# A ring of expert weights cut into 22 half-matrix tensors instead of 11 whole ones

## What is computed

```python
def routed_experts(xf, expert_idx, gates, w1, w3, w2):
    ...                      # sort the 1024 (token, expert) pairs by expert
    def expert_block(args):
        xb, e = args
        return (jax.nn.silu(xb @ w1[e]) * (xb @ w3[e])) @ w2[e]
    ...                      # gate, and add each token's two results
def hierarchical_moe(h, router_group, router_expert, w1, w3, w2):
    ...                      # top 1 of 4 groups, then top 2 of its 8 experts
    return routed_experts(xf, expert_idx, gates, w1, w3, w2).reshape(b, t, d)
```

## Time and profile before

| | |
|---|---|
| median of 3 runs | 2085.11 us (2085.02 to 2099.13) |
| the profiled execution | 2079.74 us, of which the span from first to last instruction is 2078.0 us |
| granted TensorE clock, mean | 0.905 of full speed |
| PE / PEld busy | 1707.9 us (82%) / 945.1 us (45%) |
| DVE / ACT / POOL busy | 678.9 us (33%) / 421.1 us (20%) / 173.4 us (8%) |
| HBM read / written | 461.24 MB / 23.46 MB |
| SP's queue (q1) | 86688 packets, 454.97 MB |

### The profile page before, as it was taken

One profiled execution on the slowest core, in us unless ns is written; L12 is line 12 of the kernel. 1 busy time (PEld: TensorE's weight loads), 2 busy tenths in 40 slices (PEclk: granted clock), 3 DMA queues, 4 the chain that ended last, 5 costly groups with the idle time before them and its releaser, 6 DMA issues. The chain is left out here.

```text
span 2078.0 us, 22342 instructions
## 1 busy us (share of the span) xinstructions
PE 1707.9 (82%) x8688; PEld 945.1 (45%) x8817; DVE 678.9 (33%) x1098; ACT 421.1 (20%) x725; POOL 173.4 (8%) x205
## 2 busy tenths in 40 slices
PE   7999679998794998888888499988949888888883
PEld 5775268886442333333333267854423333333331
DVE  5432966666613111111111353296221111111113
ACT  5224322222511110000000232274101100000001
POOL 0001611221101000000000100054010000000001
PEclk9999789998797999999999799999979999999996
DMA  5301000002085999999999632012759999999994
GB/s 163 102 21 21 1 1 1 1 1 82 6 325 203 360 408 405 406 407 401 405 398 399 227 106 81 15 68 60 317 216 377 399 405 403 410 403 405 396 386 167
DMA packets 99722, 486.18 MB, mean 234 GB/s; under 512 B 30912, under 2 KB 55488, under 8 KB 74528
## 3 DMA queue, kind: packets, MB, share of 16 engines
q1 hardware_dynamic: 86688, 454.97, 56.0%
q0 software_dynamic: 4736, 17.17, 2.2%
q10 hardware_dynamic: 8192, 12.59, 1.9%
HBM read 461.24 MB, written 23.46 MB: 233 GB/s over the span
## 5 line engine op out<-in xcount | busy, mean ns | idle before, releaser
L617 PE MATMUL ps<-w_unit,xT 128*48 128x512 f32 x1024 | 513.1, 660 | 132.5 <-DMA w_unit<-in_moe_w 129.9
L618 PE MATMUL ps<-w_unit,xT 128*48 128x512 f32 x1024 | 514.1, 661 | 0.0
L617 PEld LDWEIGHTS ps<-w_unit,xT 128*48 128x48 f32 x1024 | 134.0, 135 | 481.4 <-issue 478.3
L656 DVE TENSOR_TENSOR xT<-ps,gain 128x384 f32<-128x384 f32 x64 | 35.7, 557 | 730.2 <-PE ps L607 730.2
L646 PE MATMUL ps<-w_unit,hidT 128*48 128x512 f32 x512 | 238.6, 610 | 3.9 <-ACT hidT L673 3.0
L647 PE MATMUL ps<-w_unit,hidT 128*48 128x512 f32 x512 | 238.7, 610 | 0.0
L673 ACT ACTIVATE hidT<-ps 128x192 f32<-128x192 f32 x64 | 21.1, 330 | 630.4 <-PE ps L638 628.1
L1067 PE MATMUL ps<-hT_high,w_high 128*128 128x512 f32 (+1 forms) x344 | 137.9, 401 | 9.7 <-PE ps L1069 6.1
L1069 PE MATMUL ps<-hT_high,w_low 128*128 128x512 f32 (+1 forms) x344 | 135.6, 394 | 0.0
L1068 PE MATMUL ps<-hT_low,w_high 128*128 128x512 f32 (+1 forms) x344 | 134.9, 392 | 0.0
L618 PEld LDWEIGHTS ps<-w_unit,xT 128*48 128x48 f32 x1024 | 134.0, 135 | 0.0
(11 more groups left out here) (336 smaller groups left out, 2254.8 us busy)
## 6 DMA issues: line engine op xcount, KB each, us to landing
w_unit<-in_moe_w SPq DMA_DIRECT2D x188, 2048.0 KB, 37.2
x_rows<-sorted_rows SPq DMA_DIRECT2D x64, 192.0 KB, 40.2
expert_rows<-y ACTq DMA_DIRECT2D x128, 96.0 KB, 7.5
w_raw<-in_od_w_qkv SPq DMA_DIRECT2D x12, 1024.0 KB, 5.3
w_raw<-in_ev_w_in SPq DMA_DIRECT2D x10, 1024.0 KB, 5.2
w_unit<-in_moe_w SPq DMA_DIRECT2D x8, 1024.0 KB, 37.7
w_unit<-in_ev_w_out SPq DMA_DIRECT2D x2, 2048.0 KB, 11.8
w_unit<-in_od_w_out SPq DMA_DIRECT2D x2, 2048.0 KB, 10.9
```

The costliest lines, as they stand in the source:

```text
L617: nc.tensor.matmul(ps_1[b][0:MB, :], xT[b][:, k, :], w1[:, k, :], start=k == 0, stop=k == KD - 1)
L618: last = nc.tensor.matmul(ps_3[b][UP:UP + MB, :], xT[b][:, k, :], w3[:, k, :], start=k == 0, stop=k == KD - 1)
```

## The change

The ring becomes 22 tensors of 8 KB per partition, 1 MB each, of the same total size. Every matrix is now two pieces, in the order w1 first half, w3 first half, w1 second half, w3 second half, w2 first half, w2 second half (`PARTS`). Each piece has its own load, its own semaphore, and is waited for and released by itself: `up` waits for the first halves at its first step and for the second halves at its fifth, `down` for the halves of w2 at its first and third step, and a new semaphore `half_done` counts the up products that are half done, so that the first halves of w1 and w3 are free from there. The output projection's weights lie in units 16 to 19, by halves too. The last expert's pieces keep their order: w2, then first halves, then second halves.

```diff
 SLOTS = 3
-UNIT, UNITS = KD * FF, 11
-PARTS = (KD, KD, KF)
-GUEST = (8, 9)
+UNIT, UNITS = KD * FF // 2, 22
+GATE, UP_, DOWN = range(3)
+PARTS = ((GATE, 0), (UP_, 0), (GATE, 1), (UP_, 1), (DOWN, 0), (DOWN, 1))
+ROWS = (KD // 2, KD // 2, KF // 2)
+GUEST = (16, 17, 18, 19)
...
-    def load_whole(self, eng, e, part, j):
-        k = PARTS[part]
-        eng.dma_start(self.unit[j][:, :].rearrange("p (k n) -> p k n", k=k),
-                      expert(self.dram[part], e, k)).then_inc(self.landed[j], 16)
...
+    def load_part(self, eng, e, part, j):
+        which, half = PARTS[part]
+        k = ROWS[which]
+        eng.dma_start(self.view(j, part), expert(self.dram[which], e, 2 * k)[:, half * k:(half + 1) * k, :]
+                      ).then_inc(self.landed[j], 16)
...
-    def up(pe, n, b, w1, w3, first_half, second_half):
+    def up(pe, n, b, w1, w3, landed):
         pe.wait_ge(xT_out, n + 1)
         for k in range(KD):
-            if k == 0:
-                first_half()
-            if k == KD // 2:
-                second_half()
-            nc.tensor.matmul(ps_1[b][0:MB, :], xT[b][:, k, :], w1[:, k, :], start=k == 0, stop=k == KD - 1)
-            last = nc.tensor.matmul(ps_3[b][UP:UP + MB, :], xT[b][:, k, :], w3[:, k, :],
+            half, row = divmod(k, KD // 2)
+            if row == 0:
+                landed(2 * half)
+                landed(2 * half + 1)
+            nc.tensor.matmul(ps_1[b][0:MB, :], xT[b][:, k, :], w1[half][:, row, :], start=k == 0, stop=k == KD - 1)
+            last = nc.tensor.matmul(ps_3[b][UP:UP + MB, :], xT[b][:, k, :], w3[half][:, row, :],
                                     start=k == 0, stop=k == KD - 1)
-        last.then_inc(up_done, 1)
+            if row == KD // 2 - 1:
+                last.then_inc(up_done if half else half_done, 1)
...
         for k in range(KF):
...
+            half, row = divmod(k, KF // 2)
+            if row == 0:
+                landed(4 + half)
...
                 gone, was = divmod(len(PARTS) * n + part - UNITS, len(PARTS))
-                sp.wait_ge(down_done if was == 2 else up_done, gone + 1)
+                sp.wait_ge((half_done, half_done, up_done, up_done, down_done, down_done)[was], gone + 1)
...
-            for part in (0, 1, 2):
+            for part in range(len(PARTS)):
                 freed(LAST, part)
-            wts.load(sp, [len(PARTS) * LAST + 2])
-            for half in range(2):
-                for part in (0, 1):
-                    wts.load_half(sp, LAST, part, half)
+            wts.load(sp, [len(PARTS) * LAST + part for part in (4, 5, 0, 1, 2, 3)])
```

More of the change, by code:

```diff
@@ L193, in start @@
     def start(self, block):
-        w = self.wts.guest()
         @block.sync
@@ L518, in add_units, with view, of_expert @@
             self.unit[j] = self.c.sb(f"w_unit{j}", [P, UNIT], ctx=ctx, side="right")
-    def view(self, n, part):
-        return self.unit[place(n, part)[0]][:, :].rearrange("p (k n) -> p k n", k=PARTS[part])
+    def view(self, j, part):
+        return self.unit[j][:, :].rearrange("p (k n) -> p k n", k=ROWS[PARTS[part][0]])
+    def of_expert(self, n, which):
+        return [self.view(place(n, part)[0], part) for part in range(len(PARTS)) if PARTS[part][0] == which]
     def load(self, eng, pieces):
@@ L526, in load @@
             n, part = divmod(piece, len(PARTS))
-            self.load_whole(eng, n, part, place(n, part)[0])
-    def load_whole(self, eng, e, part, j):
-        k = PARTS[part]
-        eng.dma_start(self.unit[j][:, :].rearrange("p (k n) -> p k n", k=k),
-                      expert(self.dram[part], e, k)).then_inc(self.landed[j], 16)
[L534 to L539, removed]
+            self.load_part(eng, n, part, place(n, part)[0])
+    def load_part(self, eng, e, part, j):
[3 more added lines that the diff above has]
+                      ).then_inc(self.landed[j], 16)
     def arrived(self, pe, n, part):
@@ L639, in turn_hidden, with down @@
         last.then_inc(hidT_done, 1)
-    def down(pe, n, w2):
+    def down(pe, n, w2, landed):
         pe.wait_ge(hidT_out, n + 1)
@@ L645, in down @@
         for k in range(KF):
[L646 to L647 removed]
+            half, row = divmod(k, KF // 2)
+            if row == 0:
+                landed(4 + half)
+            nc.tensor.matmul(ps_y0[0:MB, :], hidT[:, k, :], w2[half][:, row, 0:FF], start=k == 0, stop=k == KF - 1)
+            last = nc.tensor.matmul(ps_y1[UP:UP + MB, :], hidT[:, k, :], w2[half][:, row, FF:D],
+                                    start=k == 0, stop=k == KF - 1)
         last.then_inc(down_done, 1)
     def down_expert(pe, n):
[L651 to L652 removed]
+        down(pe, n, wts.of_expert(n, DOWN), lambda part: wts.arrived(pe, n, part))
     def gain_rows(dve, n, b):
@@ L776, in landed, with extra @@
                     pe.wait_ge(wts.landed[EXTRA[part]], 16 * m + 16 * (LOADS[EXTRA[part]] + 1))
-                def extra(part):
-                    return wts.unit[EXTRA[part]][:, :].rearrange("p (k n) -> p k n", k=PARTS[part])
-                def first_half():
-                    landed(0)
-                    landed(1)
+                def extra(which):
+                    return [wts.view(EXTRA[part], part) for part in range(len(PARTS)) if PARTS[part][0] == which]
                 turn_rows(pe, XSLOT, u)
-                up(pe, n, 0, extra(0), extra(1), first_half, lambda: None)
+                up(pe, n, 0, extra(GATE), extra(UP_), landed)
                 turn_hidden(pe, n)
-                landed(2)
-                down(pe, n, extra(2))
+                down(pe, n, extra(DOWN), landed)
             further(pe, more)
```

48 lines of the change are left out of this document (22 added, 26 removed).

## The result

The changed kernel takes 2104.04 us in the median of 7 runs (2099.97 to 2113.25), the kernel before 2085.11 us (7 runs, 2080.01 to 2099.13). The ratio is 1.0086 with a 95% interval of 1.0056 to 1.0115: 0.9% slower, where 0.5% was forecast (2096 us, range 2083 to 2106).

A forecast was written before the change was run, and what follows sets the result against it. The prediction took the gapless stream of weight loads, plus a PE tail, to bound both stages. Per layer, 7.6 us slower stream minus 2.0 us shorter tail, twice, gave +11.2 us: 2085.1 + 11 = 2096 us, range 2083 to 2106.

The forecast's parts named there:

- Part 1: Weight stream: 8 KB pieces instead of 16 KB lower the rate from 428 to 420 GB/s, +7.6 us a layer.
- The rival in which halves mend these stretches: Where rows and results share the engines with weights, shorter packets recover lost rate; not slower, 2081 us; chance 0.17.
- Part 2: Start of a stage: earlier w2 of expert 3 fills the first gap, the second grows as much; nothing gained.
- Part 3: Steady part: earlier starts and releases by halves do not shorten a never-dry stream; PE's idle time only moves; zero.
- Part 4: Tail behind the last bytes: up(30) starts earlier, rows of expert 31 cap the gain at 2.0 us a layer.
- The sign that the prediction named: Tail: from the last landing to the end of up(31) some 3.4 us, not 6.
- Part 5: Instructions: 94 more SP loads a layer, 40 us, covered by 319 us of waiting; PE's extra waits put at 0.
- The half-deep queue: SP's load queue counts DMAs or packets, so holds only 7.5 MB; waits could outlast it, 2150 us; chance 0.06.
- The fixed price per DMA: Weight loads: the page's 2 us per DMA is partly exposed, a tenth of 163 us a layer, 2129 us; chance 0.03.

The follow-up runs named there:

- The single and double DMAs: Kernel before with 8 KB runs by one DMA per matrix (1.0100) or two (1.0106), and with 16 KB runs by two (1.0014).
- the kernel with a busy PE: The changed kernel plus 40 matmuls on zeros ahead of turn_rows for the last experts (n from 27 on): 2109.76 us, ratio 1.0090.

## Why the prediction came out as it did

**Bound and direction: right.** The stream of weights bounds both stages, it has no gap in its steady part before or after, and shorter runs slow it. The single and double DMAs show that it is the run and not the number of DMAs. In all these kernels a run is also one packet of the profile, so the two are not told apart.

**Part 1: right in kind, and likely mis-sized: +7.6 us a layer forecast, +10.3 and +10.5 in the traces, +10.4 by the ratio of the kernel with 8 KB in one DMA (1.0100 of 2089 us, halved).** The pure rates came out as read (428 and 420). The term left out was anything beyond the pure rate. That there is such a cost is shown with 4 KB runs (48 us where the pure rate gives 35); with 8 KB it is likely but each kernel's interval still holds 7.6 us a layer. The traces' +10.3 and +10.5 do not size it either, since the kernel with two DMAs of 16 KB shows +17.0 and +5.1 in its profile with no loss in the median. Where the extra time lies stays open. The prediction took the mixed stretches as unchanged, and they do not clearly lose more: by bins of 1 us, the time lost below the usual rate from 700 to 1150 us is 25 us before, 27 after, 31 and 33 in the two kernels with 8 KB runs and old waits, 34 with 4 KB, but also 32 with two DMAs of 16 KB; from 1600 to 2020 us, in layer 1, it is 26, 27, 25, 27, 29 and 28 in the same order. The rival in which halves mend these stretches (0.17) did not come.

**Part 2: right.** The first gap is filled and the second is longer; no gain shows.

**Part 3: right.** The idle time moved before turn_rows, as said, for rows that lie behind w2 in the queue, and the stage did not notice.

**Part 4: right as far as turn_rows, wrong from there on; 2.0 us a layer forecast, 0.9 and 1.5 in the traces, and these came from another place.** All of the following is counted from the last weight packet, layers 0 and 1. Turn_rows(31) started 1.95 and 1.86 us earlier than before, just as forecast. The step that failed was "with the 12.0 us from there to up(31)": a pause of 2.45 us now stands before turn_rows, the low clock that used to fall on up falls on the down products behind it (0.66 over 14 us, window below), and the way took 14.5 and 13.8 us. So up(31) started 0.5 us later and 0.05 us earlier than before, and nothing of the 2.0 us reached it.

```profile
1157.00:1171.00 14.00, 12.50 (x42) 4.29 (x45) 1.94 (x3) 0.92 (x2) 0.00 (x0) 0.66 0.90 372
```
```profile
1142.50:1154.50 12.00, 10.46 (x44) 4.32 (x47) 1.95 (x3) 1.72 (x4) 0.00 (x0) 0.86 0.87 361
```

The first line is after, the second the same way before. The sign that the prediction named did not come either: from the last weight packet to the end of up(31) it took 6.9 and 6.3 us after, 6.4 and 6.3 before, and not 3.4. What did shorten is the stretch from the start of up(31) to the end of the stage, 14.8 us before and 13.4 after in both layers, because the low clock no longer fell on its down products (the window before, then after):

```profile
1154.51:1169.30 14.79, 12.74 (x54) 4.44 (x51) 1.39 (x2) 1.51 (x3) 0.00 (x0) 0.88 0.05 16
```
```profile
1171.45:1184.80 13.35, 11.34 (x54) 3.54 (x51) 1.39 (x2) 1.51 (x3) 0.00 (x0) 1.00 0.06 16
```

The prediction had no term for that; that the sum of the tail came out near the forecast is luck. The same stretch took 13.4 us in both layers of the kernel with two DMAs of 16 KB, which has no halves. In the four profiles of kernels with whole waits and unchanged rows (before, 8 KB by one and by two DMAs, 16 KB by two) the tail runs from 11.6 to 15.8 us, 14.2 in the mean, so the 0.9 and 1.5 us are no larger than its spread.

**Part 5: right.** 94 more loads a layer are covered: SP's waits for down products fell from the 319 us of the earlier trace rows to 39.7 us, while the issue of a weight load grew from 0.43 to 2.14 us in the median: SP now stands at its queue.

```profile
SPq L535 <- PE ps L649: 39.7, 5, 11.1
```

**The half-deep queue** did not come: 28.2 us at 395 GB/s are 11 MB ahead, less than the 15 of before and more than the 7.5 feared, and the DMA share shows no gap. The queue did become shallower, then, and the other kernels show that this goes with the run too: a weight load lands after 37.2 us before, 33.6 with two runs of 8 KB in one DMA, 26.9 with two DMAs of 8 KB runs, 25.6 with runs of 4 KB. **The fixed price per DMA** of the Trainium skill ("DMA: Bandwidth & Descriptors", section "Anatomy of one DMA — SWDGE (gpsimd) path", where the prediction named the section Bandwidth) is given there for single DMAs that GpSimd issues. For the full queue of SP it is not seen here: 94 more DMAs a layer with 16 KB runs cost 0.14%, within the interval of no change.

**Sum.** 2 x (7.6 - 2.0) = 11 us forecast; 2 x (10.4 - 1.2) = 18 us in the traces, and 0.86% of 2085, 18 us, by the ratio. Both misses point the same way and are inside the bounds that were given, but for the rate, whose upper bound was 9.5. The whole came out inside the range (2104 of 2083 to 2106 us), near its upper end, with the main term right in kind and the tail's gain right only in its sum.

What stays open is why 48 partitions of rows cost three times their bytes. The shape matters (24 us in layer 0), and the time is lost in the packets of weights beside the rows. The split into 32 and 16 partitions gives back 7 us in all, and no run here tells why the weights are slowed.

## What to carry to other kernels

Where a queue of DMAs is kept full, as here, the length of the contiguous run of a partition (4 to 16 KB) sets the rate, and the number of DMAs (2 MB or 1 MB each) does not. So leave a tensor's runs whole. If it must be cut, the cut by partitions cost nothing here, though no run waits for such parts one by one; and no run shows a gain in time from finer waits, not even at the last two experts alone. Read the pure rate of both forms from the trace and add a margin, since 4 KB runs lost a third more than the pure rate says. Do not size a term of 5 us from one pair of profiles: the streams of two kernels whose medians agree differed by 17 us in one stage of their profiles. Where a forecast moves work past a pause, ask also which products the low clock will fall on next. Where the stream is the bound, look for small transfers beside it: they can cost several times their bytes.

## What the runs showed of the hardware

- Streams of weights with nothing beside them, by bins of 1 us from 700 to 1150 us: 424 to 427 GB/s with 16 KB per partition in one run, 417 to 420 with 8 KB, 409 with 4 KB.
- Rows of 4 KB on 48 partitions beside the stream cost 85 us for 11 MB; cut to 32 B a row they cost nothing that shows (426 GB/s). With them 8% of the 16 KB packets of weights from 700 to 1100 us take over 750 ns instead of 614, nearly all within 1 us of a packet of rows; with the same rows on 128 partitions 16 of 9714 do.
- TensorE's clock went low at or soon after pauses of 1.5 to 3 us (in the kernel before 2.80 us ahead of up(29) and 1.50 us ahead of down(30), in the changed one 2.45 us ahead of turn_rows(31)), though not after each (a pause of 1.62 us in the kernel with a busy PE was followed by products at full clock). It slows what comes next: up in the kernel before (L617 660 ns, L646 610 ns in the mean), down after (L624 592 ns, L648 805 ns). The way from turn_rows(31) to up(31) takes 10.3 us at a clock of 1.00, 12.0 at 0.86, 13.8 at 0.75 and 14.5 at 0.67.

```profile
L617 PE MATMUL ps<-w_unit,xT 128*48 128x512 f32 x1024 | 513.1, 660 | 132.5 <-DMA w_unit<-in_moe_w 129.9
L646 PE MATMUL ps<-w_unit,hidT 128*48 128x512 f32 x512 | 238.6, 610 | 3.9 <-ACT hidT L673 3.0
```
```profile
L624 PE MATMUL ps<-w_unit,xT 128*48 128x512 f32 x1024 | 453.8, 592 | 9.4 <-DMA w_unit<-in_moe_w 6.4
L648 PE MATMUL ps<-w_unit,hidT 128*48 128x512 f32 x512 | 329.4, 805 | 4.0 <-ACT hidT L675 4.0
```
